# A top-16 expert layer on one core: five of nine tiles leave the 8 KB row gathers, three for separate u and v gathers, two for a dense pass

## The reference, cut to what matters

```python
def block(xb):                                            # xb: 128 tokens x 1024
    q = (xb @ w_query).reshape(128, 8, 2, 128)            # 8 retrieval heads, two half keys
    s = einsum('thpd,hpkd->thpk', q, sub_keys)            # 128 keys for each half
    sv, si = top_k(s, 16)
    cand = sv[:, :, 0, :, None] + sv[:, :, 1, None, :]    # 16 x 16 sums
    cidx = si[:, :, 0, :, None] * 128 + si[:, :, 1, None, :]
    fv, fi = top_k(cand, 16)
    eidx = take_along_axis(cidx, fi)                      # 16 of 16384 experts per head
    g = softmax(fv)
    a = einsum('thkd,td->thk', expert_u[eidx], xb)        # 128 dots per token
    w = g * gelu(a)
    return einsum('thk,thkd->td', w, expert_v[eidx])
```

## Time and profile before

| | |
|---|---|
| median of three runs | 3683.46 us (3683.14 to 3683.57) |
| the profiled execution, span from the first to the last instruction | 3684.3 us |
[...]
| busy share of the span: PE, DVE, ACT, POOL | 86%, 63%, 20%, 30% |
| indirect gathers: number, bytes | 1152, 1208 MB |
| first dot of the PEER stage | 740 us |

### The profile page before, as it was taken

The page is one execution under the profiler, slowest core; times in us unless marked ns, Lnnn a source line. Parts: engine busy times, 40 slices in busy tenths (PEclk is TensorE's granted clock), DMA queues, the critical chain, the costliest instruction groups (busy, mean ns, idle before and its releaser), DMA issues.

```text
span 3684.3 us, 48012 instructions
## 1 busy us (share of the span) xinstructions
PE 3158.2 (86%) x17895; PEld 1389.9 (38%) x17895; DVE 2311.1 (63%) x6107; ACT 719.1 (20%) x2373; POOL 1110.6 (30%) x1177
## 2 busy tenths in 40 slices
PE   6999999889888878988887898889788888977776
PEld 3545556634334324423432343344234334422222
DVE  1333343867757866775776677677667757765444
ACT  2434434311111111111111111111111111111111
POOL 0000000033333333333333333333333333333332
PEclk8999999799999999999999999999999999999999
DMA  5000114299999999999999999999999999999997
GB/s 217 24 29 23 35 34 169 91 401 421 421 421 419 418 414 417 413 414 420 415 414 420 416 414 415 417 418 416 412 417 416 416 416 418 413 414 420 419 418 326
DMA packets 192682, 1275.60 MB, mean 346 GB/s; under 512 B 21056, under 2 KB 24768, under 8 KB 44608
## 3 DMA queue, kind: packets, MB, share of 16 engines
q0 software_dynamic: 165888, 1208.03, 79.4%
q1 hardware_dynamic: 26560, 64.49, 4.9%
HBM read 1260.12 MB, written 12.32 MB: 345 GB/s over the span
## 4 chain that ended last, share of the span: by engine, by line
DMA 46%; PE 35%; DVE 9%; issue 5%; POOL 4%; ACT 1%; SPq 0%; DVEq 0%; POOLq 0%; ACTq 0%
DMA arena<-in_experts,arena 45%; PE PS L1353 10%; PE PS L1182 8%; PE PS L1367 7%; POOL arena L651 4%; DVE arena L976 4%; PE PS L1276 3%; PE PS L1166 2%; PE PS L1399 2%; PE PS L1265 1%; PE PS L1225 1%; DVE arena L1051 1%; DVE arena L1054 1%; DVE arena L1057 1%; PE PS L1205 0%
## 5 line engine op out<-in xcount | busy, mean ns | idle before, releaser
L1353 PE MATMUL PS<-arena 128*128 128x512 bf16 x6912 | 1655.6, 382 | 453.1 <-DVE arena L976 440.6
L976 DVE CUSTOM_DVE_ANT_0 arena<-arena,PS 128x1024 f32<-128x1024 f32 x1152 | 1396.2, 1221 | 871.7 <-DMA arena<-in_experts,arena 548.4
L651 POOL DMA_INDIRECT arena<-in_experts,arena x1152 | 1089.0, 945 | 1938.0 <-PE PS L1367 1572.7
L1353 PEld LDWEIGHTS PS<-arena 128*128 128x128 bf16 x6912 | 611.5, 98 | 1480.5 <-DVE arena L976 865.1
L1367 PE MATMUL PS<-arena 128*32 128x512 f32 x4608 | 558.8, 603 | 16.8 <-ACT arena L867 16.8
L861 ACT ACTIVATE arena<-arena 128x4 f32<-128x4 f32 x288 | 59.5, 207 | 2156.2 <-DVE arena L976 2137.0
L1182 PE MATMUL PS<-arena 128*128 128x512 f32 (+1 forms) x720 | 309.8, 567 | 13.9 <-DMA arena<-in_w_in 7.9
L1399 PEld LDWEIGHTS PS<-arena 128*128 128x128 f32 x2304 | 266.6, 192 | 101.5 <-issue 101.5
L1399 PE MATMUL PS<-arena 128*128 128x128 f32 x2304 | 289.7, 280 | 0.0
L867 ACT ACTIVATE arena<-arena 128x1 f32<-128x1 f32 x1152 | 245.5, 284 | 9.4
L1367 PEld LDWEIGHTS PS<-arena 128*32 128x32 f32 x4608 | 120.8, 109 | 313.9 <-issue 175.4
(11 more groups left out here) (124 smaller groups left out, 1526.8 us busy)
## 6 DMA issues: line engine op xcount, KB each, us to landing
arena<-in_experts,arena POOLq DMA_INDIRECT x1152
arena<-in_w_in SPq DMA_DIRECT2D x8, 1024.0 KB, 11.8
arena<-in_w_query SPq DMA_DIRECT2D x4, 2048.0 KB, 16.1
arena<-in_xT SPq DMA_DIRECT2D x9, 512.0 KB, 3.9
h_scratch<-arena SPq DMA_DIRECT2D x9, 512.0 KB, 2.9
arena<-h_scratch SPq DMA_DIRECT2D x9, 512.0 KB, 8.1
out<-arena SPq DMA_DIRECT2D x9, 512.0 KB
arena<-in_x_prompt SPq DMA_DIRECT2D x8, 512.0 KB, 3.5
```

The lines of the kernel that those rows point to most:

```text
L651: pool.indirect_dma_start(out=uv[r], out_offset=None, in_=experts, in_offset=bass.IndirectOffsetOnAxis(ap=expert_T[t % 2][:, tok:tok + 1], ...
L976: dve.tensor_tensor_reduce(uv[r][:, 0:D], uv[r][:, 0:D], xb(n), 1.0, 0.0, ALU.mult, ALU.add, a_dot[(n // 4) % 2][:, n % 4:n % 4 + 1]).then ...
L1353: mm = pe.matmul(PS[:, 2 + 2 * (n % 2) + c, :], pick[:, tok:tok + 1].broadcast_to([P, P]), parts[t % 2][k][:, 512 * c:512 * c + 512], star ...
```

## The change

The PEER stage is cut into two parts, and the tiles are taken in another order.

Part one, units 0 to 127: tiles 0, 1, 3 and 5 (`B_TILES`) go on as before, with the same gathers, ring, `spread_x`, dots and weighing (`weigh_rows`). In those 128 units all eight remaining tiles are routed, one started every 16 units (`ROUTE_AT`), so two routings for each tile's 32 units. `deal` lays a routing out over 24 units: `norm` in its unit a, `x2T` in a+1, the q steps of round k two at a time in units a+2+4k and a+3+4k, `keys` in the next, the DVE selection of the round in four units from a+5+4k, `gates` in a+21, `turn` and `turned` in a+22 and a+23. The routing steps of ACT, `norm` and `gates` too, now stand behind the unit's gelu and weights in ACT's list (`row_gates`, then `route`).

Part two, units 128 to 255 and three more: tiles 6, 7 and 8 (`D_TILES`) are gathered as u and v apart, 4 KB rows, 512 KB for each gather. The u gather is by slot: partition p holds an expert of token p, so that x lies in SBUF as it is (`xrow`), no spreading is needed, and a dot reads two SBUF operands. Gelu and gate are then taken once for a tile, the weights are turned, and v is gathered by token as before, 35 units behind u. Tiles 2 and 4 (`PAIR`) are computed densely beside them: for 128 blocks of 128 experts, SP streams 512 KB of a transposed copy of U (`uT`, made on the host) and 512 KB of V; PE makes the 128 x 256 activations (8 float32 matmuls of 256 columns), ACT gelu, DVE the product with a dense gate matrix G, and PE adds to four PSUM banks (4 float32 matmuls of 512 columns). G is made in two bursts of 64 groups of four tokens: DVE makes one-hot rows (`spots`: four TENSOR_SCALAR 128x128 and one TENSOR_TENSOR 128x256), PE multiplies them (4 matmuls of 64 columns), ACT copies the result. `BURST_AT` and `BLOCKS_AT` say in which units that happens.

The core of the diff:

```diff
+B_TILES = (0, 1, 3, 5)
+PAIR = (2, 4)
+D_TILES = (6, 7, 8)
+RING, FIRST_BLOCK = 10, 4
+D_AT = FOURS * len(B_TILES)
+UNITS = D_AT + FOURS * (len(D_TILES) + 1)
+U_RING, E_RING = 8, 8
+LAG = 3
+ROUTE_AT = (None,) + tuple(16 * r for r in range(8))
...
+def deal():
     pe, act, dve = {}, {}, {}
...
+    for t in range(1, NT):
+        a = ROUTE_AT[t]
+        act.setdefault(a, []).append((t, "norm"))
+        dve.setdefault(a, []).append((t, "norm"))
+        if t in B_TILES:
+            dve.setdefault(a + 2, []).append((t, "split_high"))
+            dve.setdefault(a + 3, []).append((t, "split_low"))
+        pe.setdefault(a + 1, []).append((t, "x2T"))
+        act.setdefault(a + 1, []).append((t, "x2T"))
+        for k in range(4):
+            at = a + 2 + 4 * k
+            for l in range(4):
+                pe.setdefault(at + l // 2, []).append((t, "q", k, l))
+            act.setdefault(at + 1, []).append((t, "q", k))
+            pe.setdefault(at + 2, []).append((t, "keys", k))
+            act.setdefault(at + 2, []).append((t, "keys", k))
+            spent, length = 0, sum(STEP_LENGTH[s[0]] for s in steps(k))
+            for s in steps(k):
+                dve.setdefault(at + 3 + 4 * spent // length, []).append((t, *s))
+                spent += STEP_LENGTH[s[0]]
+        dve.setdefault(a + 20, []).append((t, "shift"))
+        act.setdefault(a + 21, []).append((t, "gates"))
+        dve.setdefault(a + 21, []).append((t, "gates"))
+        pe.setdefault(a + 22, []).append((t, "turn"))
+        dve.setdefault(a + 23, []).append((t, "turned"))
...
+BURST_AT = ((D_AT + 9, 13), (D_AT + 66, 10))
+BLOCKS_AT = ((D_AT + 22, 10, 10), (D_AT + 32, 32, 54), (D_AT + 76, 20, 38), (D_AT + 96, 26, 26))
+DENSE = {}
+for j, (begin, units) in enumerate(BURST_AT):
+    for g in range(GROUPS):
+        DENSE.setdefault(begin + g * units // GROUPS, []).append(("scatter", j, g))
+b = 0
+for begin, units, blocks in BLOCKS_AT:
+    for i in range(blocks):
+        DENSE.setdefault(begin + i * units // blocks, []).append(("block", b))
+        b += 1
+assert b == NKEYS
...
+T_RING = 3
+ACT_RING, W_RING, BEHIND = 2, 4, 2
...
+COLLECT_AT = [FOURS * (i + 1) for i in range(len(B_TILES))]
+COLLECT_AT += [D_AT + FOURS * (i + 2) + LAG for i in range(len(D_TILES) - 1)] + [DENSE_END + 2] * 2 + [UNITS + LAG]
+SQUARES, SCALE_LAST, STORE = 4, 5, 6
...
+                def load_uT(b):
+                    if b == 0:
+                        sp.wait_ge(key_psum, 4 * NT)
+                    if b == 2:
+                        sp.wait_ge(row_used, D_AT)
+                    if b >= T_RING:
+                        sp.wait_ge(act_psum, b - T_RING + 1)
+                    sp.dma_start(uT_ring[b % T_RING].rearrange("p k j -> p (k j)"), expert_uT[b * P:(b + 1) * P, :])\
+                      .then_inc(uT_in[b % T_RING], 16)
+
+                def load_v(b):
+                    if b >= T_RING:
+                        sp.wait_ge(dense_done, b - T_RING + 1)
+                    sp.dma_start(v_dense[b % T_RING], expert_v[b * P:(b + 1) * P, :]).then_inc(v_in[b % T_RING], 16)
...
+                for n in range(UNITS - D_AT + LAG):
+                    s, f = split(n)
+                    if s < len(D_TILES):
+                        if f == 0:
+                            pool.wait_ge(routed, s + 1)
+                        for g in range(4):
+                            m = 4 * n + g
+                            if m in (0, 2):
+                                pool.wait_ge(row_used, D_AT - 2 + m // 2)
+                            if m >= U_RING:
+                                pool.wait_ge(dots_ready, m - U_RING + 1)
+                            o = 4 * f + g
+                            pool.indirect_dma_start(
+                                out=u_ring[m % U_RING], out_offset=None, in_=expert_u,
+                                in_offset=bass.IndirectOffsetOnAxis(ap=eidx_u[s][:, o:o + 1], axis=0))\
+                                .then_inc(u_in[m % U_RING], 16)
+                    v = n - FOURS - LAG
+                    if v >= 0:
+                        s, f = split(v)
+                        if f == 0:
+                            pool.wait_ge(turned, D_TILES[s] + 1)
+                        if v == 0:
+                            pool.wait_ge(row_used, D_AT)
+                        if v >= 2:
+                            pool.wait_ge(four_used, v - 1)
+                        for g in range(4):
+                            m, tok = 4 * v + g, 32 * g + f
+                            pool.indirect_dma_start(
+                                out=e_ring[m % E_RING], out_offset=None, in_=expert_v,
+                                in_offset=bass.IndirectOffsetOnAxis(ap=expert_D[s][:, tok:tok + 1], axis=0))\
+                                .then_inc(e_in[m % E_RING], 16)
...
+                for u in range(D_AT):
+                    row_gates(u)
+                    for t, step, *k in ACT_AT.get(u, ()):
+                        route(t, step, *k)
+                    for n in range(NT):
+                        if u == COLLECT_AT[n] + SQUARES:
+                            squares(n)
...
+                def dot(s, o):
+                    n = u_slot(s, o)
+                    r = n % U_RING
+                    dve.wait_ge(u_in[r], rows_in(r) + 16 * (n // U_RING + 1))
+                    if o == 0:
+                        dve.wait_ge(xrow_in[s % 2], 16 * (s // 2 + 1))
+                    dve.tensor_tensor_reduce(u_ring[r], u_ring[r], xrow[s % 2], 1.0, 0.0, ALU.mult, ALU.add,
+                                             a_dot[s % 2][:, o:o + 1]).then_inc(dots_ready, 1)
...
+                def spots(j, g):
+                    n = GROUPS * j + g
+                    if n >= 2:
+                        dve.wait_ge(scatter_psum, n - 1)
+                    t0 = P * (g // FOURS) + 4 * (g % FOURS)
+                    for k in range(4):
+                        dve.tensor_scalar(hot_j[n % 2][:, k, :], iota, j_T[:, t0 + k:t0 + k + 1], g_T[:, t0 + k:t0 + k + 1],
+                                          ALU.is_equal, ALU.mult).then_inc(hot_ready, 1)
+                    dve.tensor_tensor(hot_i[n % 2], iota[:, HALF * j:HALF * (j + 1)].unsqueeze(1).broadcast_to([P, 4, HALF]),
+                                      i_T[:, t0:t0 + 4].unsqueeze(2).broadcast_to([P, 4, HALF]), ALU.is_equal).then_inc(hot_ready, 1)
+
+                def gate_dense(b):
+                    dve.wait_ge(act_ready, b + 1)
+                    dve.wait_ge(G_ready, GROUPS * (b // HALF + 1))
+                    if b >= W_RING:
+                        dve.wait_ge(dense_done, b - W_RING + 1)
+                    dve.tensor_tensor(w_ring[b % W_RING].rearrange("p (q t) -> p q t", q=2),
+                                      act_ring[b % ACT_RING].rearrange("p (q t) -> p q t", q=2),
+                                      G[:, :, b % HALF, :], ALU.mult).then_inc(wd_ready, 1)
...
+                for u in range(D_AT):
+                    for i in range(4):
+                        row_dot(4 * u + i)
+                        for n in range(NT):
+                            if u == COLLECT_AT[n] and i == 1:
+                                collect(n)
+                            if u == COLLECT_AT[n] + SCALE_LAST and i == 0:
+                                finish(n)
+                    for t, step, *k in DVE_AT.get(u, ()):
+                        route(t, step, *k)
...
+                    for i in range(4):
+                        if s < len(D_TILES):
+                            dot(s, 4 * f + i)
+                        if s and f == 0 and i == 0:
+                            weights(s - 1)
+                        if s and f == 1 and i == 1:
+                            weights_turned(s - 1)
+                        for n in range(NT):
+                            if u == COLLECT_AT[n] and i == 0:
+                                collect(n)
+                            if u == COLLECT_AT[n] + SCALE_LAST and i == 0:
+                                finish(n)
+                        for kind, *k in dense[len(dense) * i // 4:len(dense) * (i + 1) // 4]:
+                            if kind == "scatter":
+                                spots(*k)
+                            else:
+                                gate_dense(*k)
...
+                def weigh_experts(v):
+                    s, f = split(v)
+                    if v == 0:
+                        pe.wait_ge(row_dots, SLOTS * len(B_TILES))
+                    if f == 0 and s:
+                        pe.wait_ge(acc_free, len(B_TILES) + s)
+                    pe.wait_ge(wz_ready, v + 1)
+                    for g in range(4):
+                        m = 4 * v + g
+                        pe.wait_ge(e_in[m % E_RING], 16 * (m // E_RING + 1))
+                    for c in range(2):
+                        for g in range(4):
+                            r = (4 * v + g) % E_RING
```

(45 more changed lines are left out.)

639 lines of the change are left out of this document (434 added, 205 removed).

## The result

The changed kernel takes 3800.2 us (3795.2 to 3801.5) against 3683.5 for the kernel before: a ratio of 1.031, 95% interval 1.030 to 1.032, slower by 117 us. The forecast was 3724, slower by 40. The direction came out as said, the size did not: 76 us are missing. The time lies in the range of 3600 to 3870, but outside the forecast's own 3695 to 3775.

A forecast was written before the change was run, and what follows sets the result against it. The PEER stage, bound by its gathers before, would be bound in part one by the engines' handshake: 740 us before the stage, 1477 for part one and 1507 for part two make 3724 us; own range 3695 to 3775, 8-in-10 range 3600 to 3870.

The forecast's parts named there:

- four units of selection: Part one: four units holding one selection round, two q steps in each of two units, and keys take 42.5 us.
- the seven other stretches: Part two outside both bursts and the end, each costed by the engine or DMA that sets it: 1161 us.
- turning weights and uneven units: Part two: turning the weights three times, 9 us, and uneven units in the DMA-bound stretches, 12 us.
- the first two find their x spread, the others wait for PE, which takes 1.39 a spread: Handshake of a unit: with PE free early, four dots take 5.24 us; four spreads take 5.56.
- Rival 1: Part one: the handshake costs nothing, so part one takes 1402 us and the total 3649, faster; chance 0.20.
- DVE 10 x 4.6 + 83: Second burst, units 66-75: DVE's work sets the pace; with 4 for collect and finish, 133 us (DMA 102).
- 36 for 122-130, v alone, two units of it ahead: End of part two: units with only v gathers, two of them already ahead, take 36 us.
- The port: Part two: gather issues meeting two-operand DVE instructions can alternate with them; nothing added beyond 1.3 us for a group.
- rival 3: Bursts: DVE doesn't let POOL in between back-to-back instructions, so issues add 164 less 14; total 3874; chance 0.13.
- rival 2: Part one: the ring hides norm and gates waits too, 4 x (321 + 10) = 1324, total 3571; chance 0.05.
- rival 5: Whole kernel: part two's gain and part one's loss cancel within 0.2%; chance 0.07.
- rival 4: Part two: 4 KB rows run at 357 GB/s, about +120 us where DMA bounds, total 3844; chance 0.07.

The follow-up runs named there:

- run 12: Changed kernel with 16 small unread matmuls on PE in each part-one unit without a routing step: 3778.1 us, ratio 1.025.
- run 1: Changed kernel with ScalarE's norm and gates put ahead of the unit's gelu and weights in part one: 3742.7 us, ratio 1.016.
- run 4: Changed kernel with two extra float32 matmuls on PE ahead of each scatter group's four, to keep PE busy in the bursts: 3792.3 us, ratio 1.029.
- run 9: Changed kernel leaving out two of the four TENSOR_SCALAR of each one-hot group: 3749.6 us, ratio 1.017.
- run 5: Changed kernel with three instead of two buffers for the one-hot rows: 3789.0 us, ratio 1.028.
- run 3: Changed kernel with the last 26 dense blocks laid over 32 units instead of 26: 3805.1 us, ratio 1.033.
- run 6: Changed kernel with twelve instead of eight buffers for the last v gathers: 3784.0 us, ratio 1.027.
- run 11: Changed kernel with norm/gates ahead, q steps spread, third one-hot buffer, twelve v buffers, plus last two blocks' values in two later units: 3618.6 us, ratio 0.982.
- run 2: Changed kernel with q steps dealt 2, 1, 1 over three units, keys in the fourth, selection and what follows one unit later: 3717.2 us, ratio 1.008.
- run 8: Changed kernel with norm and gates ahead of the gelu and q steps spread 2, 1, 1 over three units: 3650.4 us, ratio 0.991.

## Why the prediction was half right

The direction and the mechanism of the loss held: the handshake bounds part one, and norm and gates are paid there. The sizes did not. The largest miss is the second burst, whose term had no wait in it; the end and the spreads of part one were costed too short. Term by term:

| step | forecast | measured | shown by |
|---|---|---|---|
| four units of selection | 42.5 | 44.0 | run 12 |
| a unit with norm, beyond that | 5.6 | 5.8 (16.6 against 10.8) | run 1 |
| wait at gates | 2.8 | 2.8 | run 1 |
| collect, squares and finish | 5.9 | 6.4 | trace |
| splits of a tile (3 and 5) | 3.7 | 0.3 and 1.9 | trace |
| the first 16 units, with split and empty buffers | 189 | 181 | trace |
| part one | 1477 | 1496 | |
| first burst | 143 | 147 | runs 4, 9 |
| the seven other stretches | 1161 | 1173 | trace |
| second burst | 133 | 165 | run 5 |
| the end, from the last block | 49 | 72 | runs 3, 6, 11 |
| turning weights and uneven units | 21 | in the others | |
| part two | 1507 | 1558 | |

**Part one (19 of 76).** The step "the first two find their x spread, the others wait for PE, which takes 1.39 a spread" was mis-sized: 1.39 is the spread at the upper clock (5.56 for four at 1.00). In most units that follow one without a PE step the engine had just stood 2.96 us, the clock was lower, and four spreads took 7.04 (0.83 from 1230.4 to 1240.4). The prediction had the lower clock in mind for the bursts and the end, not here. This term alone doesn't make the 19. A routing's 16 units took 184.8 instead of 180.4, so the seven routings behind the first cost 31 more, and the first 16 units and the splits gave 13 of them back, by luck. Of the 4.4 up to 2.8 lie in the second eight units (84.7 to 87.8, forecast 85.0), where the clock is the cause: with PE kept busy they take 84.5 to 85.7. The first eight, which also hold norm and gates, take 97.3 to 99.3 in the four routings without a finish, where 95.4 was forecast, and in run 12 still 97.5 to 98.5; why stays open. Rival 1, a free handshake at 1402, was wrong for this order of steps. With another, run 2 comes to 1414, and run 8, without the waits for ScalarE, to 1348: its point that the spare time is there was true, only the two q steps in one unit kept it from being used.

**Part two, second burst (32).** The failed step is "DVE 10 x 4.6 + 83": it counts DVE's own work, which was about right (137.7 busy, with the finish), and no wait. The trace has 32 us of waits in three places. First, the burst was costed like the first one, but beside it PE weighs v, 1.9 to 3.6 us a unit in one piece and ahead of the scatters in its list, and two one-hot buffers do not cover that: 14.3 us in eight waits, of which run 5 leaves one of 3.6. Second, the rows are late at the start: 5.2 for u rows and 8.3 for PE, which itself waits 7.0 for v rows; run 5 leaves 5.7 of the 8.3, and what makes the rows late, beyond a full DMA just before, no run asked. Third, 4.3 are for ScalarE in the finish, of which the forecast had 4 for collect and finish together. How much of the 14.3 is the lower clock, at which a weighing takes 3.64 (granted 0.50 from 3152.66 to 3156.30) instead of 1.92, run 4 does not settle.

**The end (23).** "36 for 122-130, v alone, two units of it ahead" took such a unit at DMA's 5.1. With two units of buffers it is the round trip, 7, and the two units ahead could not grow into more while PE stood in the last values. Run 6 confirms the first (13 us in its trace), run 11 by its trace the second (7).

**The port.** The trace shows how long the issues and the dots that meet take, not what they share. The forecast added nothing beyond 1.3 for a group, and rival 3 would have added 150. In the first burst a dot with a group takes 2.52, against 1.15 + 1.3 in the forecast:

```profile
2393.71 1.21 DVE L1269 CUSTOM_DVE_ANT_0 arena<-arena 128x1024 f32<-128x1024 f32 x1
...
2394.86 1.33 DVE L1289 TENSOR_SCALAR arena<-arena 128x128 f32<-128x128 f32 x4
2395.21 0.93 POOL L858 DMA_INDIRECT arena<-in_expert_u,arena  x1 [1.59 <-DVE arena L1269]
2395.90 0.41 DVE L1291 TENSOR_TENSOR arena<-arena 128x256 f32<-128x256 f32 x1
```

Beside an issue the four take 1.33, alone 1.10 (2389.84). In such a pair that is all DVE loses; it is POOL that pays, up to 2.20 for an issue that meets a dot. In the lines of run 5 such an issue ends only 0.81 us behind the dot; the price is one-sided in the meetings seen, 0.2 us for DVE (1.33 against 1.10) and 1.3 for POOL (2.20 against 0.94). Rival 3 is refuted by both bursts, which took 36 more than forecast together and not 150. Rivals 2 and 5 did not occur, nor did rival 4: the stretches bound by DMA run at 405 to 410 GB/s. The 1.28 us that the forecast took for 0.524 MB no row shows, only the 1.27 to 1.47 around it; at 405 to 410 GB/s it is 1.28 to 1.29.

## What to carry to other kernels

Before work is added to a stage, ask what the engines' own handshake (each waiting for the other's last step) takes without the transfer that hides it: here 10.6 to 11.0 us a unit under a DMA pace of 10.0, enough to turn 10% fewer bytes (1148 MB on the two queues instead of 1273) into a longer kernel. There every wait is paid in full (57 us for what cost nothing before), and evening out the lumps is worth more than removing work: moving a quarter of the q steps and reordering ScalarE's list gave 150 us with not one instruction less. When an engine is costed as full, list what its partner does in one piece in the same unit, count how much time the buffers between them cover, and ask whether the rows for the stretch's first unit are there.

## What the runs showed of the hardware

Behind the same 2.96 us of idle PE the granted clock fell in one unit (0.83, 24 matmuls in 7.04 us) and not in another (1.00, 5.56). So the same gap of 3 us went once with 1.5 us more for the matmuls behind it and once with none, in an engine that is 87% busy over the span. With PE kept busy the granted clock rose from 0.50 to 0.97 in the first burst and from 0.64 to 0.95 in the second (run 4), and from 0.94 to 0.97 in part one (run 12). The two runs also show that the clock was worth something only where PE was the late one: 22 us in part one, nothing in the first burst, where a unit took 11.4 at either level. In the second burst run 4 doesn't tell, as its added matmuls took up what the clock gave.

In the second burst 17 gather issues beside a dot with two SBUF operands took 1.93 to 2.21 us instead of 0.94, more than the 1.63 of the earlier trace rows. They met it nearer to its start: 1.63 began 0.47 us into such an instruction, 1.93 (at 3150.31) 0.10 into the dot, and 2.20 (at 3152.54) 0.18 ahead of it. In the lines of run 5, as in the earlier trace rows, the issue ended some 0.8 us behind that instruction's end: the one at 3152.54 lasts to 3154.74, the dot at 3152.72 to 3153.93. An issue beside one-operand TENSOR_SCALAR took 0.93 (2395.21). The median issue took 0.94 with 4 KB rows (L858, L873) as with 8 KB rows (L841). The 4 KB rows cost little against 8 KB ones: 405 to 410 GB/s where DMA set the pace (gathers alone or with streamed blocks), against 412 to 421, or 1.28 to 1.29 us for 0.524 MB.
